# Later modulation vectors as row products on VectorE, an earlier norm sum, and filler matmuls in two waits of an encoder layer

## The reference

```
mod = silu(c) @ w_ada + b_ada
sh1, sc1, g1, sh2, sc2, g2, sh3, sc3, g3 = split(mod, 9)
h = rms_norm(x, ffn1_norm) * (1 + sc1) + sh1
x = x + 0.5 * g1 * swiglu(h, ffn1_w1, ffn1_w3, ffn1_w2)        # D_FF = 2816
h = rms_norm(x, mix_norm) * (1 + sc2) + sh2
z = h @ w_in                                                    # 3584 columns
y = concat(hgrn2(z), rglru(z)) @ w_out                          # two bidirectional recurrences
x = x + g2 * y
h = rms_norm(x, ffn2_norm) * (1 + sc3) + sh3
x = x + 0.5 * g3 * swiglu(h, ffn2_w1, ffn2_w3, ffn2_w2)
return rms_norm(x, final_norm)
```

## Time and profile before

| | us |
|---|---|
| median of 3 runs | 1109.04 |
| lowest, highest of them | 1106.64, 1111.95 |
| the profiled execution | 1112.39 |
| its span, first to last instruction | 1110.6 |

### The profile page before, as it was taken

One profiled execution on the slowest core, in us unless ns is written; L12 is line 12 of the kernel. 1 busy time (PEld: TensorE's weight loads), 2 busy tenths in 40 slices (PEclk: granted clock), 3 DMA queues, 4 the chain that ended last, 5 costly groups with the idle time before them and its releaser, 6 DMA issues.

```text
span 1110.6 us, 13888 instructions
## 1 busy us (share of the span) xinstructions
PE 1069.1 (96%) x4996; PEld 873.0 (79%) x4996; DVE 585.5 (53%) x692; ACT 407.1 (37%) x521; POOL 151.8 (14%) x143
## 2 busy tenths in 40 slices
PE   7999999999999999998998898999999999999997
PEld 5678888888888888777785767878888888888886
DVE  4467777743422227569799899463333333322313
ACT  5232222222312223585774674343222222321211
POOL 0011111100000110026463433100000000000100
PEclk9999999999999999998998899999999999999999
DMA  9558888722232223221111111212222332222222
GB/s 357 217 176 270 259 281 274 257 90 94 95 101 96 100 81 140 76 76 58 57 58 39 57 57 39 76 52 100 94 96 98 104 99 94 94 95 94 95 94 76
DMA packets 37426, 132.44 MB, mean 119 GB/s; under 512 B 4112, under 2 KB 4368, under 8 KB 37264
## 3 DMA queue, kind: packets, MB, share of 16 engines
q1 hardware_dynamic: 29024, 100.83, 26.4%
q0 software_dynamic: 8368, 31.13, 8.5%
HBM read 129.85 MB, written 2.10 MB: 119 GB/s over the span
## 4 chain that ended last, share of the span: by engine, by line
PE 85%; DVE 9%; issue 3%; ACT 3%; DMA 0%; DVEq 0%; SPq 0%; ACTq 0%
PE psum L1239 25%; PE psum L1241 25%; PE psum L1240 24%; PE psum L1543 2%; PE psum L1557 2%; PE psum L1513 1%; PE psum L1352 1%; DVE qk L1088 1%; PE psum L1276 1%; DVE wlo L735 1%; DVE qk L1087 1%; PE psum L1345 1%; PE psum L1484 1%; PE psum L1486 1%; PE psum L1485 1%
## 5 line engine op out<-in xcount | busy, mean ns | idle before, releaser
L735 DVE TENSOR_TENSOR wlo<-raw,whi 128x1024 fp32r<-128x1024 f32 x166 | 209.3, 1261 | 336.4 <-ACT whi L376 336.1
L376 ACT ACTIVATE whi<-raw 128x1024 fp32r<-128x1024 f32 x164 | 173.7, 1059 | 546.3 <-PE psum L1241 538.5
L1239 PE MATMUL psum<-hhi,whi 128*128 128x512 f32 x896 | 359.1, 401 | 12.0 <-DVE sg L1039 5.4
L1240 PE MATMUL psum<-hlo,whi 128*128 128x512 f32 x896 | 351.4, 392 | 0.0
L1241 PE MATMUL psum<-hhi,wlo 128*128 128x512 f32 x896 | 351.3, 392 | 0.0
L1239 PEld LDWEIGHTS psum<-hhi,whi 128*128 128x128 f32 x896 | 170.2, 190 | 55.9 <-issue 10.9
L1241 PEld LDWEIGHTS psum<-hhi,wlo 128*128 128x128 f32 x896 | 169.6, 189 | 36.2
L1240 PEld LDWEIGHTS psum<-hlo,whi 128*128 128x128 f32 x896 | 170.2, 190 | 35.0 <-issue 1.4
L1239 PE MATMUL psum<-ghi,whi 128*128 (+1 forms) x352 | 138.5, 394 | 0.0
L1241 PE MATMUL psum<-ghi,wlo 128*128 (+1 forms) x352 | 138.1, 392 | 0.0
L1240 PE MATMUL psum<-glo,whi 128*128 (+1 forms) x352 | 136.8, 389 | 0.0
(11 more groups left out here) (188 smaller groups left out, 968.7 us busy)
## 6 DMA issues: line engine op xcount, KB each, us to landing
raw<-wu SPq DMA_DIRECT2D x168, 512.0 KB, 3.3
ada<-wada POOLq DMA_DIRECT2D x56, 512.0 KB, 4.9
early<-wada SPq DMA_DIRECT2D x16, 512.0 KB, 14.8
x<-xt SPq DMA_DIRECT2D x4, 512.0 KB, 5.5
out<-outt SPq DMA_DIRECT2D x8, 256.0 KB, 2.2
bd<-bd POOLq DMA_DIRECT2D x1, 1024.0 KB, 5.3
dif<-consts POOLq DMA_DIRECT2D x1, 448.0 KB, 5.9
resets<-consts POOLq DMA_DIRECT2D x1, 256.0 KB, 6.5
```

The source lines that it names most:

```text
L376: nc.scalar.activation(whi[:, slot, :], raw[:, slot, :], ACT.Copy).then_inc(hi_done, 1)
L735: nc.vector.tensor_tensor(wlo[:, slot, :], raw[:, slot, :], whi[:, slot, :], ALU.subtract).then_inc(lo_done, 1)
L1239: nc.tensor.matmul(dst, a, rhi, start=start, stop=False)
L1240: nc.tensor.matmul(dst, a, rlo, start=False, stop=False)
```

## The change

Four things change.

1. DVE now computes the seven later vectors alone. `w_ada`'s later part is laid out transposed, so that a tile `ada` has 128 output features on the partitions and the 1024 input features along the row. `csr` holds silu(c) repeated on all 128 partitions. `ada_row(j, k)` multiplies the tile by `csr`, in place, and sums the row into one column of `modt`. `mod_rows(j)` adds the bias to eight such columns. `mod_sum` on PE is gone, with `acc`, `fin` and the semaphore between them, and the PE list of FFN1's up steps becomes one loop.
2. `c_rows` (512 KB) is a new input. POOL loads it ahead of the `ada` tiles, and ACT applies silu to it in `up_step(0, 1)`, behind the silu of the product.
3. At the start PE takes the second half of the norm sums ahead of `block_rows(0, 0)`, with three `keep_busy` in front of it and two behind; there were two in front of the rows and four behind the sums.
4. PE runs `keep_busy(3, 3)` in front of `block_sums(0)`, and `keep_busy(3, 8)` behind `block_rows(1, 0)` and behind `block_rows(2, 0)`. Bank 3 is free there.

```diff
@@ -135,8 +134,9 @@
         sq0, _ = at("sq0", [P, KD, T], F32, off)
         ada, off = at("ada", [P, 4, D], F32, off)
         rows, _ = at("rows", [P, 2, T], F32, off)
-        acc, off = at("acc", [P, D], F32, off)
-        fin, off = at("fin", [P, D], F32, off)
+        off += 4 * D
+        csr, off = at("csr", [P, D], F32, off)
+        modt, off = at("modt", [P, KD], F32, off)
         outt, _ = at("outt", [P, KD, T], F32, arena)
 
         yhi, _ = at("yhi", [P, KD, T], F32R, h_at)
...
@@ -308,6 +308,7 @@
 
             pool.wait_ge(sq_used, 3)
             pool.wait_ge(first_loaded[-1], 16)
+            pool.dma_start(csr[:], c_rows).then_inc(c_loaded, 16)
             for k in range(8):
                 if k >= 4:
                     pool.wait_ge(ada_added, k - 3)
@@ -436,6 +437,9 @@
                 if not (isinstance(f, int) and KF * n + f == 0):
                     act.wait_ge(gate_prod, f + KF * n)
                 nc.scalar.activation(silu_sb[:], bank[fp], ACT.Silu).then_inc(silu_done, 1)
+                if isinstance(f, int) and KF * n + f == 1:
+                    act.wait_ge(c_loaded, 16)
+                    nc.scalar.activation(csr[:], csr[:], ACT.Silu).then_inc(csr_done, 1)
                 if not is_early:
                     hi(j + 1, 1)
                 elif f:
...
@@ -739,26 +742,21 @@
                 if u < N_UNITS:
                     lo(u // 2, u % 2)
 
-            def ada_add(j, k):
+            def ada_row(j, k):
 
                 dve.wait_ge(ada_loaded[k % 4], 32 * j + (16 * (k // 4 + 1) - 64))
-                if not (isinstance(j, int) and j == 2 and k == 0):
-                    dve.wait_ge(ada_added, 8 * j + (k - 16))
-                dst = acc
-                if k == 7:
-                    dst = fin
-                    if not (isinstance(j, int) and j == 2):
-                        dve.wait_ge(mod_summed, j - 2)
                 if k == 0:
-                    nc.vector.tensor_scalar(dst[:], ada[:, k % 4, :], cs[:, k:k + 1], None,
-                                            ALU.mult).then_inc(ada_added, 1)
-                else:
-                    nc.vector.scalar_tensor_tensor(dst[:], ada[:, k % 4, :], cs[:, k:k + 1], acc[:], ALU.mult,
-                                                   ALU.add).then_inc(ada_added, 1)
-
-            def mod_bias(j):
-                dve.wait_ge(mod_summed, j - 1)
-                nc.vector.tensor_tensor(mods[:, bass.ds(8 * j, 8)], modp, vecs[:, bass.ds(8 * j + VEC["b_ada"], 8)],
+                    if isinstance(j, int) and j == 2:
+                        dve.wait_ge(csr_done, 1)
+                    else:
+                        dve.wait_ge(mod_ready, j - 2)
+                nc.vector.tensor_tensor_reduce(ada[:, k % 4, :], ada[:, k % 4, :], csr[:], 1.0, 0.0, ALU.mult, ALU.add,
+                                               modt[:, k:k + 1]).then_inc(ada_added, 1)
+
+            def mod_rows(j):
+
+                dve.wait_ge(ada_added, 8 * j - 8)
+                nc.vector.tensor_tensor(mods[:, bass.ds(8 * j, 8)], modt[:], vecs[:, bass.ds(8 * j + VEC["b_ada"], 8)],
                                         ALU.add).then_inc(mod_ready, 1)
 
             def add_first_squares(i):
@@ -835,7 +833,7 @@
                 if after_first:
                     lo(j + 1, 0)
                 for k in ks[0:2]:
-                    ada_add(mod_j, k)
+                    ada_row(mod_j, k)
                 dve.wait_ge(unit_used, 2 * j + 2)
                 dve.wait_ge(silu_done, f + (KF * n + 1))
                 if not (isinstance(f, int) and KF * n + f == 0):
...
@@ -967,14 +965,12 @@
                 up_step(0, fp, fp, 0)
             for fp in range(2):
                 up_step(0, 2 + fp, fp, 1, 2)
+            mod_rows(2)
             with dve.Fori(2, 8) as i:
                 for fp in range(2):
                     up_step(0, 2 * i + fp, fp, i, i + 1)
-                mod_bias(i)
-            for fp in range(2):
-                up_step(0, 16 + fp, fp, 8)
-            mod_bias(8)
-            with dve.Fori(9, KF // 2) as i:
+                mod_rows(i + 1)
+            with dve.Fori(8, KF // 2) as i:
                 for fp in range(2):
                     up_step(0, 2 * i + fp, fp, i)
             ffn_down(0)
@@ -1267,16 +1263,6 @@
                         ins = three(bank[2 * s + fp], s, k * P, hhi[:, k, :], hlo[:, k, :], k == 0, k == KD - 1)
                     ins.then_inc(unit_used, 1)
 
-            def mod_sum(j):
-
-                pe.wait_ge(ada_added, 8 * j - 8)
-                if not (isinstance(j, int) and j == 2):
-                    pe.wait_ge(mod_ready, j - 2)
-                for t in range(KD):
-                    ins = nc.tensor.matmul(modp[:, t:t + 1], fin[:, t * P:(t + 1) * P], ones[:, 0:1], start=True,
-                                           stop=True)
-                ins.then_inc(mod_summed, 1)
-
             def down_unit(half, slot, rhs, first, last, wait_for):
 
                 wait_for()
@@ -1420,19 +1406,22 @@
 
             keep_busy(7, 26)
             first_norm_sums(0)
+            keep_busy(7, 3)
+            first_norm_sums(1)
+            block_rows(0, 0)
             keep_busy(7, 2)
-            block_rows(0, 0)
-            first_norm_sums(1)
-            keep_busy(7, 4)
             norm_rb(0)
             block_rows(0, 1)
+            keep_busy(3, 3)
             block_sums(0)
             block_rows(1, 0)
+            keep_busy(3, 8)
             first_unit(0, range(0, 2))
             block_rows(1, 1)
             first_unit(1, range(0, 2))
             block_sums(1)
             block_rows(2, 0)
+            keep_busy(3, 8)
             first_unit(0, range(2, 4))
             block_rows(2, 1)
             first_unit(1, range(2, 4))
...
@@ -1447,16 +1436,7 @@
                 first_unit(u, range(4, 6))
             for u in range(4):
                 first_unit(u, range(6, 8))
-            for fp in range(2):
-                up_step(0, 2 + fp, fp, 1)
-            up_step(0, 4, 0, 2)
-            mod_sum(2)
-            up_step(0, 5, 1, 2)
-            with pe.Fori(3, 9) as i:
-                up_step(0, 2 * i, 0, i)
-                mod_sum(i)
-                up_step(0, 2 * i + 1, 1, i)
-            with pe.Fori(9, KF // 2) as i:
+            with pe.Fori(1, KF // 2) as i:
                 for fp in range(2):
                     up_step(0, 2 * i + fp, fp, i)
             ffn_down(0)
@@ -1673,9 +1653,10 @@
     units.append(_block_units(np.concatenate([w_out[T:], w_out[:T]]), OUT_BLOCKS))
     ffn(i["ffn2_w1"][0], i["ffn2_w3"][0], i["ffn2_w2"][0])
     order = [MOD_AT[m] for m in MODS]
-    wada = i["w_ada"][0].reshape(KD, P, N_MOD, D).transpose(2, 0, 1, 3)[order].reshape(N_MOD * KD, P, D)
-    head = wada[:2 * KD].reshape(2, 4, 2, P, BLOCKS, 2 * P).transpose(4, 1, 3, 2, 0, 5).reshape(4 * BLOCKS, P, D)
-    wada = np.concatenate([head, wada[2 * KD:]])
+    w = i["w_ada"][0]
+    head = w.reshape(4, 2, P, N_MOD, BLOCKS, 2 * P)[:, :, :, order[:2]].transpose(4, 0, 2, 1, 3, 5)
+    rows = w.reshape(D, N_MOD, KD, P).transpose(1, 2, 3, 0)[order[2:]]
+    wada = np.concatenate([head.reshape(4 * BLOCKS, P, D), rows.reshape((N_MOD - 2) * KD, P, D)])
     vecs = [_cols(i["c"][0]), _cols(i["b_ada"][0].reshape(N_MOD, D)[order].reshape(-1)),
             _cols(i["ffn1_norm"][0]), _cols(i["mix_norm"][0]), _cols(i["ffn2_norm"][0]), _cols(i["final_norm"]),
             _cols(i["hg_lb_fwd"][0]), _cols(i["hg_lb_bwd"][0]), _cols(i["hg_lb_fwd"][1]), _cols(i["hg_lb_bwd"][1]),
...
@@ -1694,7 +1675,8 @@
     resets[:, ::P] = 0.0
     return {
         "xt": np.ascontiguousarray(i["x"][0].T), "wu": np.ascontiguousarray(np.concatenate(units)),
-        "wada": np.ascontiguousarray(wada), "vecs": np.ascontiguousarray(np.concatenate(vecs, axis=1)),
+        "wada": np.ascontiguousarray(wada),
+        "c_rows": np.ascontiguousarray(np.broadcast_to(i["c"][0], (P, D))), "vecs": np.ascontiguousarray(np.concatenate(vecs, axis=1)),
         "bd": bd, "consts": np.concatenate([np.eye(P, dtype=np.float32), resets, mask.reshape(P, 7 * P)], axis=1),
     }
 
```

More of the change, by code:

```diff
@@ L78, with build @@
 N_VEC = _at
-def build(nc, xt, wu, wada, vecs_in, bd_in, consts_in, out):
+def build(nc, xt, wu, wada, c_rows, vecs_in, bd_in, consts_in, out):
     with ExitStack() as ctx:
@@ L108, in build @@
         epst = sb("epst", [P, 1])
-        cs = sb("cs", [P, KD])
         cs32 = sb("cs32", [P, KD, COLUMNS])
@@ L174, in build @@
         bank = [psum[:, b, :] for b in range(8)]
-        modp = psum[:, 5, 0:8]
         def modq(q):
@@ L484, in _ @@
             nc.scalar.activation(cs32[:, :, 0], vec("c", 0, 8), ACT.Silu).then_inc(cs_done, 1)
-            nc.scalar.activation(cs[:], vec("c", 0, 8), ACT.Silu).then_inc(cs_done, 1)
             nc.scalar.preload_act_table(ACT.Sqrt)
@@ L919, in small_values @@
             def small_values():
-                dve.wait_ge(cs_done, 4)
+                dve.wait_ge(cs_done, 3)
```

3 lines of the change are left out of this document (2 added, 1 removed).

## The result

The changed kernel takes 1093.63 us (median of 4 runs, 1092.83 to 1094.86), the kernel before 1110.49 in the same comparison (4 runs, 1106.64 to 1113.3). The ratio is 0.9854 with a 95% interval of 0.9832 to 0.9876: 1.5% faster, which is 16.2 us by the ratio and 16.9 by the medians. The forecast was 1095 us and lies 1.4 us off. Its gain was 14.0 us, counted from an earlier median of 1109.04, so the gain is off by more than the time. In the profiled executions it is 1112.39 against 1093.68, which is 18.7 us where the prediction's sum had 14.7. The 4.0 us in between are the interesting part.

The account below looks back on a forecast made before the run. PE, busy without a gap in FFN1's up steps, was taken as the bound. The sums' 12.5 us plus 1.5 of the start's net 2.2 gave 1109.0 - 14.0 = 1095 us, with an 8 in 10 range of 1090 to 1103.

Parts of the forecast that it names:

- Part 1: FFN1's up steps: seven `mod_sum` at 1.79 us each leave PE's path, 12.5 us gained.
- Part 2: FFN1's up steps: DVE's new product with sum takes 1.28 to 1.44 us, hidden behind PE, so costs nothing.
- The scan's 2.59: Upper estimate for DVE's new operation, 2.59 us for 1024 elements, from the scan that carries a value between elements.
- slack of 3.1 us: Time in an up step between `wlo` on DVE being ready and PE turning to the next unit, 3.1 us.
- the threshold at which DVE binds: FFN1's up steps: DVE starts to bind at 1.76 us an operation; the whole gain is eaten at 2.07 us.
- Part 3: At the start, POOL's load of `c_rows` (0.6 us) and ACT's silu (about 1.06 us) are hidden, costing nothing.
- Part 4: At the start, norm sums ahead of `block_rows(0, 0)` make the first root later, +0.6 us on the path.
- Part 5: At the start, fillers in PE's gaps keep the clock up and bring back 2.8 us.
- the two thirds: Share of the start's net 2.2 us gain carried from the profiled to a median execution, 1.5 us.
- the first (fillers that don't hold the clock): Rival at the start: the clock falls despite fillers, 1097 to 1099 us; chance 0.26 together with the later-waits rival.
- The second (DVE as the bound): Rival in FFN1's up steps: operations of 2.35 us make DVE the bound, 1125 us, 1139 at 2.59; chance 0.08.
- The third (later waits take some back): Rival in FFN1's up steps: seven step pairs each lose 0.3 us, 1097 us; chance 0.26 together with the fillers rival.

Follow-up runs that it names:

- experiment 5: The changed kernel with eight one-column matmuls, result unread, put back on PE at the seven places of the old sums: 1106.49 us, ratio 0.9966.
- experiment 6: The changed kernel with half of DVE's row products done twice, six operations per up step instead of four: 1092.84 us, ratio 0.9846.
- experiment 7: The changed kernel with all of DVE's row products done twice, eight operations per up step instead of four: 1119.55 us, ratio 1.0087.
- experiment 3: The kernel before with only the new order, norm sums ahead of the first rows, and no fillers: 1112.84 us, ratio 1.0023.
- experiment 2: The kernel before with the new start alone, norm sums first and all three filler sets: 1110.04 us, ratio 0.9989.
- experiment 1: The changed kernel with the old start, no bank 3 fillers and norm sums in the old order: 1094.5 us, ratio 0.9844.
- experiment 9: The changed kernel with an unused 64-byte tile where `cs` stood, giving `ghi` and `glo` their old addresses: 1096.37 us, ratio 0.9874.
- experiment 11: The changed kernel with an unused 64-byte tile in front of all other tiles: 1093.38 us, ratio 0.9857.

## Why the prediction was right

**Part 1, the sums leave PE: right.** 12.5 us forecast, 12.6 between the two starts of the table, and with the dummies of experiment 5 12.9 by the medians and 12.4 by the ratios.

**Part 2, DVE hides its new work: right, but its range for the operation missed.** The operation took 1.22 us and 1.14 from start to start, below the low end of 1.28, under which "nothing suggests" it could run. The scan's 2.59 was no guide, and its 1404 ns is a mean of four of which the median is 1224. The slack of 3.1 us and the threshold at which DVE binds held: experiment 6, at six operations, lost nothing and experiment 7, at eight, lost 25.9 where the same sum gives 27. 1218 ns for 1024 elements is 1.19 ns an element with everything in it, where twice the multiply-add's slope would be 2.08. The Trainium skill (Vector Engine (DVE) Microarchitecture Reference, section "Points that are easy to get wrong") has half throughput for the multiply-add's layout with two SBUF sources that aren't bf16; neither the multiply-add before nor this operation ran at half. Whether the instruction, which the trace calls CUSTOM_DVE_ANT_0, has that layout is not shown. The reading of the sum is a second instruction, 56 rows of each kind; it takes 0.08 us beside the next operation and not 0.16 ahead of it. The Trainium skill's VectorE: DVE Perf Modes, section "Two Vector instructions with no wait between them", says that it is two instructions, and the trace agrees.

**Part 3, `c_rows`: right.** The load issued for 0.70 us at 37.08 and ACT's silu took 1.04 at 56.15; PE did not wait for the split behind it:

```profile
37.08 0.70 POOL L311 DMA_DIRECT2D csr<-c_rows  x1 [36.49 <-DMA early<-wada]
```

```profile
56.15 1.04 ACT L442 ACTIVATE csr<-csr 128x1024 f32<-128x1024 f32 x1
57.10 1.05 ACT L426 ACTIVATE whi<-raw 128x1024 fp32r<-128x1024 f32 x1
```

**Part 4, the order: right in sign.** +0.6 on the path forecast, +0.4 from the first norm sum to the first h matmul in the traces (experiment 3). In the changed kernel's own trace the root is at 15.64, earlier than the 16.01 before, and directly behind the copy:

```profile
15.14 0.60 ACT L414 ACTIVATE rows<-psum 128x512 f32<-128x512 f32 x1 [4.29 <-PE psum L1373]
15.64 0.26 ACT L391 ACTIVATE rms<-psum,epst 128x4 f32<-128x4 f32 x1
```

PE could begin at 3.40 and not at 4.07 there, because the first transfers landed earlier in that execution. Two traces differ by 0.7 us in this before any of the change runs, which is as much as part 4 is about. Counted from the first norm sum, the root came at 4.13 us (11.51 to 15.64) and before at 3.52 (12.49 to 16.01), so it is later by 0.6. The prediction had 1.0: it let the copy move by 1.29 us where it moved by 1.0, and the root wait for the end of the copy's 0.60 us where it starts after 0.50.

**Part 5, the fillers: the mechanism right, the size for the median not shown.** In the trace the clock stayed up and the stretch at low clock took 4.94 us and not 7.71, which is the 2.8 of the subtraction. Step 2 came 2.9 us earlier (2.2 forecast for the whole start); about 0.5 of this is the late beginning of the profiled execution before, as the two other traces with the old start have step 2 at 59.53 and 59.51. The prediction carried 1.5 us of the start over to the median. Against the kernel before, experiment 2 gives 1.2 us by the ratio, with an interval from 3.1 faster to 0.7 slower, and nothing by the medians; and between experiment 1 and the changed kernel nothing is shown either. The step that failed is the two thirds: the profiled execution, at 0.984, belongs with its clock to the group with the lowest clock and the longest times (last section), so it was no fair base for what a median execution loses. It is with the new order that the full 2.8 us come back in the median (experiments 2 and 3), and that base is 3.2 us slower than the kernel before.

**What the sum lacked: the addresses.** Dropping `cs` moved `ghi` and `glo` by 64 bytes, worth 2.2 to 2.7 us (experiment 9); in the table it stands in the two phases with down products, 1.1 and 1.2. The prediction said "no rows of `fin`" and spoke of every instruction that goes, but did not ask what the removed tile does to the places of the others. That the forecast of 1095 is closer than its parts is luck, twice: this missing term and the overestimated start partly cancel, 2.2 to 2.7 against 0.5 to 1.5, and the median of the kernel before that it subtracts from was 1.45 us lower than in the comparison that measured the change.

**The mixer's 1.5 us** go with the clock from 580 to 660 (0.89 and 0.96). From the mixer's first matmul to the last `pv` it takes 274.4 to 275.2 us in the five traces with 0.96 there and 276.0 to 276.7 in the nine with 0.89 or 0.90, with the same code. The experiments with the new vectors have 0.96 four times and 0.89 four times. The phase's place in the span doesn't decide: it begins at 403.1 in the changed kernel (0.96) and in experiment 11 (0.89). But all five traces with the old vectors have 0.89 or 0.90, so whether the change makes the higher clock likelier stays open.

Of the rivals, the first (fillers that don't hold the clock) is refuted where they stand, by the clock of ten traces. The second (DVE as the bound) is refuted by the changed kernel's trace, and experiments 6 and 7 show where it would begin. The third (later waits take some back) is refuted too: from 60 us to the end of FFN1 no wait of PE is in the changed kernel's trace, and only the one ahead of step 2 grew, from 0.86 to 1.02 us.

## What to carry to other kernels

Where PE is busy without a gap, work on one column of a 128x128 block is dear: eight such matmuls took 1.8 us here, and another engine with a third of its time to spare did the reduction at no cost in time. Ask of a removed or added tile what it moves: compare the start-to-start spacing of the same matmuls in untouched phases before you credit the change with the rest. Read what a clock gate costs from many executions, not from one profile, which may be one of the slower ones. And price two small changes of the same stretch in all four combinations: here the fillers were worth 2.8 us with one order of the norm sums and nothing with the other.

## What the runs showed of the hardware that I had not expected

**The place of the moving operand sets the matmul's spacing.** 128x512 float32 matmuls, start to start: 0.2267 us with `ghi` a multiple of 4096 bytes behind `whi`, 0.2289 with 64 more, 0.2333 with 128 more. The 4096 holds for the tiles only: the blocks that single matmuls read lie multiples of 512 bytes apart, so three distances don't give a rule. Why is not known, and whether it is the distance to the weights or to another tile that moves along wasn't tried.

**The clock makes groups of executions.** In the comparison of experiments 1 to 4 the kernel before ran 29 times: 27 times between 1106.3 and 1113.9 us, once with 1116.4 at a clock of 0.938, and once with 2759.4 that is left out of the ratios. By the mean granted clock the 27 fall apart: 0.988 to 0.990 with 1106.3 to 1107.2 us (5 runs), 0.986 to 0.988 with 1108.6 to 1109.8 (11), 0.982 to 0.985 with 1110.9 to 1113.9 (11). The kernel with fillers alone had 0.986 to 0.990 and 1107.9 to 1110.9 in all of 12, the one with the order alone 0.982 to 0.985 and 1111.1 to 1114.0. So fillers remove the worst group and the order alone gives only the worst; but the best with fillers is 1.5 us behind the best without. That they cost this much where the clock would have stayed up is one reading, and not shown: the mean clock holds the mixer's low stretches as well as the start's, and only one execution of each kernel was profiled. In the later comparisons the groups of the kernel before are less sharp (0.985 with 1109.6, 0.990 with 1108.3).

**The first matmuls are slow while the record says 1.00.** The first twelve `keep_busy` rows of the changed kernel take 2.93 us, 0.24 each; from 9.83 on fifteen take 1.84, 0.12 each. Twice the spacing is what the lower of the two levels, 1.2 GHz, would give, though the granted clock of the window from 0 to 12 us reads 1.00:

```profile
0.00:12.00 12.00, 8.60 (x58) 8.60 (x58) 4.31 (x11) 7.38 (x11) 0.20 (x4) 1.00 0.80 297
```
